# Three modulation tiles behind each projection in place of two, state-space steps to match, and constants loaded in two parts

## The chip, the cores and the metric

The kernel is one program on 1 core of a Trainium2 chip. The metric is the device time in microseconds (us) of one execution; lower is better. TensorE is called PE in the rows, VectorE DVE, ScalarE ACT, GpSimd POOL, and SyncE (which issues most of the transfers) SP. PEld is TensorE's loading of stationary operands.

## The reference: what is computed

Two transformer blocks run one after the other on 256 tokens of width 1024. The change touches only the start of the first block:

```
cs = silu(c)
mod = cs @ ada_w + ada_b              # ada_w: 1024 x 6144
sh1, sc1, g1, sh2, sc2, g2 = split(mod, 6)
h = rms_norm(x, norm1_g) * (1 + sc1) + sh1
u, q, k_cmp, v_cmp, k_slc, k_win, v_slc, v_win, gates, ... = h @ w_in
...                                    # state-space mixer on u: 32 groups, 64 states, a scan over 256 tokens
...                                    # compressed keys and values: gelu(blocks @ w1) @ w2
```

The second block has a modulation of the same shape, silu(c_2) and silu(c_ctx_2) times w_mod_2 (1024 x 6144). Its columns and the last four sixths of `mod` are needed only much later, so the kernel computes all of them here, as filler between the projections. After this stage come attention, the merging of the two branches, a mixture of experts (32 experts), and the second block with a mixture of experts of its own, which takes the larger part of the time.

## The kernel before

Every engine has an instruction stream of its own, written out in Python. The streams are tied by semaphores: `mark` counts an event up and `nth` gives the count that a waiting engine needs. The order on each engine is the order of the code, and nothing on an engine passes an instruction that waits.

**Weights.** All weights come through a ring of 12 slots of 1 MB (`RING`). The list `chunks` gives the order; `load` on SyncE waits until chunk i minus 11 has been counted as freed, and issues chunk i. First come eight chunks of modulation group 0. Then, for the 12 projections of the list `IN1` (u 0, u 1, q 0 to 3, kcmp, vcmp, kslc, kwin, vslc, vwin; below they are iterations i = 0 to 11), one chunk of `w_in` each, and behind each from i = 1 on two modulation chunks. Then a small chunk `ng`, two modulation chunks, four chunks `cw1` of the compression, and the last 16 modulation chunks. There are 40 modulation chunks in this filler, number f being k = f % 8 of group g = 1 + f // 8.

**Modulation on TensorE.** `modulation(g, k)` adds chunk k into bank 3 with four matmuls of 32 columns by 512. The sum over k = 0 to 7 is one group; ScalarE copies it out of bank 3 in `mod_rows(g)`, and TensorE turns it later in `turn_modulation(g)`. There is one bank for it, so the first matmul of the next group waits for that copy:

```
if k == 0 and g >= 1:
    pe.wait_ge(emptied, nth(emptied, ("mod rows", g - 1)))
```

**State-space steps.** The mixer has 16 steps j. `ssm_step()` on TensorE issues the input half `ssm_in(j)` of the next step and the output half `ssm_out(j)` of an earlier one, which runs two steps behind. Between them VectorE does the products and the scan of step j (L1923 to L1936), for which ScalarE makes sines (`sines()`, L1499 to L1502). ScalarE runs two calls of `sines()` ahead of TensorE's steps, and for want of buffers its call number j waits for VectorE's result of step j - 2:

```
act_.wait_ge(madeV, nth(madeV, ("fr", j)))
if j >= 2:
    act_.wait_ge(madeV, nth(madeV, ("s", j - 2)))
```

Before the change, TensorE does in each iteration from i = 2 on: the projection (L464, 128x128 by 128x256), two modulation chunks, one step, and at i = 3, 6 and 9 a second step right behind the first. ScalarE does in the same iteration: the copy of the projection out of its bank (`take`), its share of the two modulation chunks (`mod_rows` after k = 7, `mod_columns` at k = 2), and one or two calls of `sines()`.

**After the projections.** TensorE does `ng`, two modulation chunks and a step; the compression matmuls (hidR); four chunks and a step; hidT; four chunks and a step; kc; the last eight chunks; the turning of group 5; and what is left of the steps. Then VectorE adds the skip term (yD, L1939), and attention begins with two `scores` and the `router_constant`.

**Constants.** `K` is one tile of 1876 columns, loaded by one transfer at the start (938 KB); the three packs of parameters, which TensorE turns first, stand behind the constants in it. VectorE makes 16-bit copies of the identity and of two masks as its first work.

Of the kernel before, what the change touches and what calls it, by code (L numbers as in the profile page):

```python
# [19 lines left out]
P = 128  # L20
# [62 lines left out]
CONST_ARRAY = constants()  # L83
NCONST = CONST_ARRAY.shape[1]
# [22 lines left out]
def packed(I):  # L107

    packs = np.zeros((P, 3, P), np.float32)

    def rows(pk, at, name):
        a = I[name].reshape(-1, P)
        packs[at:at + len(a), pk, :] = a

    for at, name in ((0, "ada_b"), (48, "norm1_g"), (56, "norm2_g"), (64, "final_g"), (72, "nsa_cmp_pos"), (104, "c"),
                     (112, "c_2"), (120, "c_ctx_2")):
        rows(0, at, name)
    for at, name in ((0, "b_mod_2"), (48, "g_pre_mix_2"), (56, "g_post_mix_2"), (64, "g_pre_ffn_2"), (72, "g_post_ffn_2")):
        rows(1, at, name)
    for at, name in ((0, "ssm_lam_re"), (16, "ssm_lam_im"), (48, "ssm_d")):  # L120
        rows(2, at, name)
    packs[32:48, 2, :] = np.repeat(I["ssm_log_dt"].reshape(16, 2), 64, axis=1)

    ssm = np.zeros((P, 1536), np.float32)
    for n, name in enumerate(("ssm_c_re", "ssm_c_im")):
        c = I[name].reshape(4, P, 64).transpose(1, 0, 2)
        ssm[:, 512 * n:512 * n + 512] = np.concatenate([c, c], 2).reshape(P, 512)
    for n, name in enumerate(("ssm_b_re", "ssm_b_im")):
        ssm[:, 1024 + 256 * n:1280 + 256 * n] = I[name].reshape(16, P, 16).transpose(1, 0, 2).reshape(P, 256)

    by_rows = lambda a: a.reshape(-1, P, a.shape[-1]).transpose(1, 0, 2)
    tab = np.zeros((P, NTABLES), np.float32)
    tab[:, 0:288] = np.concatenate([by_rows(I["moe_w_group"]), by_rows(I["moe_w_expert"])], 2).reshape(P, 288)
    tab[:, 288:544] = by_rows(I["w_router_2"]).reshape(P, 256)
    tab[:, 544:800] = by_rows(I["nsa_cmp_w2"].reshape(512, HD)).reshape(P, 256)
    tab[:, 800:864], tab[:, 864:928] = I["g_qnorm_2"], I["g_knorm_2"]
    tab[0, 928:996] = np.concatenate([I["moe_b_group"], I["moe_b_expert"], I["b_router_2"]])
    return np.concatenate([CONST_ARRAY, packs.reshape(P, 3 * P)], 1), ssm, tab


class Counts:
# [18 lines left out]
def program(nc, A, const, ssm, tables, out, known):  # L160
# [3 lines left out]
    with ExitStack() as ctx:  # L164
# [3 lines left out]
        def sem(name):  # L168
            return ctx.enter_context(nc.semaphore(name))
# [7 lines left out]
        K = sb("consts", [P, NCONST + 3 * P])  # L177

        def cst(name, a=None, b=None):
            at, n = CONST[name]  # L180
            return K[:, at + (a or 0):at + (n if b is None else b)]

        packs = K[:, NCONST:NCONST + 3 * P].rearrange("p (a b) -> p a b", b=P)
        ring = sb("ring", [P, RING, SLOT])
        xT = sb("xT", [P, KD, T])
        hT = sb("hT", [P, KD, 2 * T])
# [9 lines left out]
        tab = sb("tables", [P, NTABLES])  # L196
# [155 lines left out]
        def mod_chunks(f, n):  # L352

            for i in range(f, min(f + n, 40)):
                mod_chunk(1 + i // 8, i % 8)
# [6 lines left out]
        for i, (n, c, at) in enumerate(IN1):  # L362
            chunk((n, c), wcols("w_in", at, at + 256), KD, 256)
            if i >= 1:
                mod_chunks(2 * i - 2, 2)
        chunk(("ng", 0), A["w_in"][:, 2560:2608].rearrange("(k p) c -> p k c", p=P), KD, 48)
        mod_chunks(22, 2)
        for kv in range(2):
            w = A["nsa_cmp_w1"][kv].rearrange("(c p) h -> p c h", p=P)
            for c in range(2):  # L370
                chunk(("cw1", kv, c), w[:, 8 * c:8 * c + 8, :], 8, 256)
        mod_chunks(24, 16)
        for c in range(4):
            chunk(("mga", c), wcols("w_in", 3120 + c * 256, 3376 + c * 256), KD, 256)
            chunk(("mgs", c), wcols("w_in", 4144 + c * 256, 4400 + c * 256), KD, 256)
# [46 lines left out]


        const_in = sem("constants_in")
        tables_in = sem("tables_in")
        ssm_loaded = sem("ssm_loaded")
        ctx_in = sem("ctx_in")
# [43 lines left out]

        @block.sync
        def _(sp):
            sp.dma_start(K[:, :], const[:, :]).then_inc(const_in, 16)

            for i in range(n1):
                key, src, shape = chunks[i]
                load(sp, key, i, src, shape)
                if key == ("u", 0):
                    sp.dma_start(arena[:, 1024:2560], ssm).then_inc(ssm_loaded, 16)  # L480
                if i == RING - 1:
                    sp.dma_start(tab[:, :], tables).then_inc(tables_in, 16)
# [101 lines left out]
        def _(pe):  # L584
# [149 lines left out]
            for i, (n, c, _) in enumerate(IN1):  # L734
                if n in ("u", "q"):
                    projT(n, c)
                elif n in ("kcmp", "vcmp", "kslc", "kwin"):
                    projT(n, 0)
                else:
                    projN(n, 256)  # L740
                freeing()
                if i == 1:
                    ssm_matrices()
                if i >= 1:
                    modulations(2)
                if n != "u":
                    ssm_step()
                    if i % 3 == 0:
                        ssm_step()
            projN("ng", 48)  # L750
            freeing()
            modulations(2)
            ssm_step()

            pe.wait_ge(emptied, nth(emptied, ("p1", turn[0] - 1)))
# [5 lines left out]
                              start=c == 0, stop=c == 15)  # L761
            last.then_inc(filled, mark(filled, "hidR"))
            freeing(4)
            modulations(4)
            ssm_step()
            pe.wait_ge(madeA, nth(madeA, "hidR"))
            for m in range(2):
                last = transpose(ps[:, 1, m * P:(m + 1) * P], hidR[:, m * P:(m + 1) * P])
            last.then_inc(filled, mark(filled, "hidT"))
            modulations(4)  # L770
            ssm_step()
            pe.wait_ge(madeA, nth(madeA, "hid"))
            pe.wait_ge(tables_in, 16)
# [5 lines left out]
                    last = mm(ps[0:NCMP, 1, g * HD:(g + 1) * HD], hid[:, m, 64 + g * NCMP:64 + (g + 1) * NCMP], w2c[:, 1, m, :],  # L779
                              start=m == 0, stop=m == 1)  # L780
            last.then_inc(filled, mark(filled, "kc"))
            modulations(8)
            turn_modulation(5)
            while done_j[1] < 16:
                ssm_step()
# [612 lines left out]
        def _(act_):  # L1398
# [107 lines left out]
            for i, (n, c, _) in enumerate(IN1):  # L1506
# [24 lines left out]
                    take(lambda b: copy((vslc if n == "vslc" else vwin)[:, :, :], two(b)))  # L1531
                if i == 1:
                    ssm_matrices()
                if i >= 1:
                    modulations(2)
                sines()
                if n != "u" and i % 3 == 0:
                    sines()
            take(lambda b: a(gates[:, :, :], b[:, 0:96].rearrange("p (a b) -> p a b", a=2), ACT.Sigmoid))
            modulations(2)  # L1540
            sines()

            act_.wait_ge(filled, nth(filled, "hidR"))
            a(hidR, ps[:, 0, 0:256], ACT.Gelu_apprx_tanh).then_inc(madeA, mark(madeA, "hidR"))
            modulations(4)
            sines()
            act_.wait_ge(filled, nth(filled, "hidT"))
            copy(hid.rearrange("p a b -> p (a b)"), ps[:, 1, 0:256]).then_inc(madeA, mark(madeA, "hid"))
            modulations(4)
            sines()  # L1550
            act_.wait_ge(filled, nth(filled, "kc"))
            copy(kcT, ps[:, 0, 0:60])
            copy(vcN[0:NCMP, :, :].rearrange("p a b -> p (a b)"), ps[0:NCMP, 1, 0:256]).then_inc(madeA, mark(madeA, "kc"))
            modulations(8)
            mod_columns(5)
            while nsin[0] < 16:
                sines()
# [244 lines left out]
        def _(v):  # L1802
# [28 lines left out]
            V.memset(cpad, 0.0)  # L1831
            v.wait_ge(const_in, 16)
            V.tensor_copy(ident16, cst("ident"))
            V.tensor_copy(causal16, cst("causal"))
            V.tensor_copy(cmpmask16, cst("cmpmask"))

            v.wait_ge(madeA, nth(madeA, "cols"))
            tt_(csil[:, :], csil[:, :], cols[:, 0, 104:128], ALU.mult)
# [44 lines left out]
            tt_(sm(12), sm(12), sm(10), ALU.mult)  # L1883
            step(tt_(sm(13), sm(14), sm(10), ALU.mult))
            b3 = lambda x: x.rearrange("p (j h) -> p j h", h=16)
            v.wait_ge(ssm_loaded, 16)
            cr_, ci_ = B(sm(12), 16), B(sm(13), 16)
            tmp = b3(sa[:, 0, :])
# [506 lines left out]
```

## Time and profile before

| | |
|---|---|
| median of 3 runs | 2052.98 us (2050.46 to 2053.23) |
| the profiled execution's own time | 2053.45 us |
| its span, first to last instruction | 2051.7 us |
| mean granted TensorE clock | 0.959 of full |
| TensorE busy | 1832.5 us (89%) |
| bytes moved | 626.77 MB, mean 305 GB/s |
| first projection begins | 33.30 us |
| attention of the first block begins | 214.72 us |

The stage that the change touches is the first tenth of the span. What lies behind attention's start does not depend on it except through the moment at which it begins. A time in the rows is microseconds from the start of the span.

### The profile page before, as it was taken

The numbers are of one execution on the slowest core, as the hardware profiler recorded it, in microseconds if no ns is written. First come the engines' busy times: TensorE is split into PE (matmuls) and PEld (weight loads), VectorE is DVE, ScalarE is ACT, GpSimd is POOL, SyncE is SP. The second block draws the span as 40 slices with busy tenths as digits, with TensorE's granted clock in tenths as the row PEclk, the third lists the DMA queues.
The fourth block names the chain that finished last, engine by engine and source line by source line (L and its number), as shares of the span: only waits on it lengthen the run. The fifth ranks groups of instructions, "written<-read, shape, count | busy, mean of one in ns | idle before, by whom it ended". The sixth has DMA issues, their size and how long they took to land.

```text
span 2051.7 us, 27907 instructions
## 1 busy us (share of the span) xinstructions
PE 1832.5 (89%) x10699; PEld 1006.3 (49%) x10700; DVE 527.4 (26%) x1211; ACT 390.7 (19%) x905; POOL 50.2 (2%) x109
## 2 busy tenths in 40 slices
PE   6999899978667889999978999889988999989887
PEld 4665677855344566777844333333333333323332
DVE  3676332131111133232431111111111111111112
ACT  3132454021011130244020111111100111101111
POOL 0040000000000010010010000000000000000000
PEclk9999899998888999999989999999999999999999
DMA  9968622418999662232435999999999899999997
GB/s 399 403 230 346 271 82 84 162 63 334 394 411 409 267 215 87 65 100 98 152 149 208 416 417 417 417 417 418 416 416 419 323 418 417 416 417 417 416 416 297
DMA packets 108632, 626.77 MB, mean 305 GB/s; under 512 B 11200, under 2 KB 15296, under 8 KB 50080
## 3 DMA queue, kind: packets, MB, share of 16 engines
q1 hardware_dynamic: 106688, 620.10, 75.1%
q0 software_dynamic: 1584, 4.33, 1.3%
q8 instruction: 70, 1.15, 0.2%
q10 hardware_dynamic: 272, 1.05, 0.1%
q14 instruction: 18, 0.15, 0.0%
HBM read 624.39 MB, written 1.05 MB: 305 GB/s over the span
## 4 chain that ended last, share of the span: by engine, by line
PE 62%; DMA 20%; SPq 10%; issue 4%; DVE 2%; ACT 1%; DVEq 0%; ACTq 0%
PE ps L464 59%; DMA ring<-in_w_gu_dram 15%; SPq L517 5%; SPq L520 4%; PE ps L592 2%; DMA ring<-in_moe_w_gate_dram 1%; DMA ring<-in_w_dn_dram 1%; DMA ring<-in_ada_w_dram 1%; DMA ring<-in_w_mod_dram 1%; DMA ring<-in_moe_w_down_dram 1%; ACT arena L1403 1%; PE ps L839 0%; SPq L490 0%; SPq L421 0%; ACT hT L1730 0%
## 5 line engine op out<-in xcount | busy, mean ns | idle before, releaser
L464 PE MATMUL ps<-ring,arena 128*64 128x512 f32 (+2 forms) x5376 | 898.8, 558 | 123.7 <-issue 59.1
L464 PEld LDWEIGHTS ps<-ring,arena 128*64 128x64 f32 (+1 forms) x5376 | 291.7, 131 | 671.4 <-issue 482.2
L464 PE MATMUL ps<-arena 64*128 64x512 f32 (+11 forms) x1494 | 262.2, 417 | 36.7 <-ACT arena L1403 15.5
L464 PE MATMUL ps<-hT,ring 128*128 128x256 f32 (+1 forms) x960 | 237.2, 402 | 2.3 <-DVE hT L1864 2.3
L464 PEld LDWEIGHTS ps<-hT,ring 128*128 128x128 f32 x960 | 180.5, 192 | 58.8 <-issue 33.6
L464 PEld LDWEIGHTS ps<-arena 64*128 64x128 f32 (+7 forms) x1494 | 128.2, 159 | 154.5 <-issue 97.0
L2212 DVE TENSOR_SCALAR arena<-ps 128x512 f32<-128x512 f32 (+1 forms) x34 | 23.0, 676 | 535.3 <-PE ps L464 535.3
L1403 ACT ACTIVATE arena<-ps 128x256 f32<-128x256 f32 (+5 forms) x191 | 104.3, 570 | 267.7 <-PE ps L592 134.0
L1669 ACT ACTIVATE arena<-ps,mod,gain 128x128 f32<-128x128 f32 x176 | 66.1, 458 | 425.3 <-PE ps L464 425.3
L1681 ACT ACTIVATE arena<-arena 128x512 f32<-128x512 f32 (+1 forms) x44 | 25.3, 575 | 601.7 <-DVE arena L2212 400.7
L464 PEld LDWEIGHTS ps<-arena,hN 128*128 128x128 f32 x960 | 116.3, 200 | 42.2 <-issue 16.3
L464 PE MATMUL ps<-arena,hN 128*128 128x128 f32 (+1 forms) x960 | 124.8, 287 | 10.3 <-DVE arena L2159 5.7
L464 PE MATMUL ps<-ring,hT 128*128 128x256 f32 (+2 forms) x416 | 83.5, 380 | 5.8 <-ACT hT L1743 5.8
L592 PE MATMUL ps<-consts,arena 128*128 128x128 f32 x522 | 73.7, 278 | 9.2 <-DVE arena L2218 6.2
L464 PEld LDWEIGHTS ps<-ring,hT 128*128 128x128 f32 (+1 forms) x416 | 70.6, 187 | 19.3 <-issue 8.3
L2199 DVE COPY arena<-ps 128x512 f32<-128x512 f32 x34 | 23.5, 692 | 214.1 <-PE ps L464 214.1
L464 PE MATMUL ps<-arena,ring 128*128 128x256 f32 x352 | 76.5, 380 | 0.7 <-ACT arena L1403 0.7
L592 PEld LDWEIGHTS ps<-consts,arena 128*128 128x128 f32 x522 | 60.1, 142 | 31.9 <-issue 15.0
L464 PEld LDWEIGHTS ps<-arena,ring 128*128 128x128 f32 x352 | 66.7, 190 | 10.3 <-ACT arena L1403 0.9
L1576 ACT ACTIVATE arena<-ps,stat 128x15 f32<-128x15 f32 (+3 forms) x128 | 56.0, 447 | 79.3 <-DVE stat L1960 79.3
L1960 DVE TENSOR_REDUCE stat<-ps 128x2 f32<-128x1024 f32 (+3 forms) x40 | 36.7, 917 | 129.4 <-PE ps L464 129.4
L464 PE MATMUL ps<-hN,ring 128*128 128x256 f32 x256 | 56.4, 380 | 0.0
(286 smaller groups left out, 876.1 us busy)
## 6 DMA issues: line engine op xcount, KB each, us to landing
ring<-in_w_gu_dram SPq DMA_DIRECT2D x256, 1024.0 KB, 20.3
ring<-in_w_dn_dram SPq DMA_DIRECT2D x128, 1024.0 KB, 23.1
ring<-dense_dram SPq DMA_DIRECT2D x56, 1024.0 KB, 12.2
ring<-in_moe_w_gate_dram SPq DMA_DIRECT2D x32, 1024.0 KB, 8.2
ring<-in_moe_w_up_dram SPq DMA_DIRECT2D x32, 1024.0 KB, 16.0
ring<-in_moe_w_down_dram SPq DMA_DIRECT2D x32, 1024.0 KB, 14.6
ring<-in_ada_w_dram SPq DMA_DIRECT2D x24, 1024.0 KB, 18.5
ring<-in_w_mod_dram SPq DMA_DIRECT2D x24, 1024.0 KB, 8.5
```

Of the source, the lines that this page charges most:

```text
L464: ins = nc.tensor.matmul(*a, start=start, stop=stop, **k)
L517: sp.dma_start(ring[:, i % RING, :], src).then_inc(full[i % RING], 16)
L520: sp.dma_start(slot_ap(i, (2, D)), src).then_inc(full[i % RING], 16)
L592: return nc.tensor.transpose(dst, src, ident[0:src.shape[0], 0:src.shape[0]])
L1403: return a(dst, src, ACT.Copy, scale=scale)
L1576: last = a(e_[:, s * nk:s * nk + m], ps[:, bank, at:at + m], ACT.Exp, bias=stat[:, i % 2, s:s + 1], accum_out=stat[:, i % 2, 4 + s:5 + s])
L1669: last = a(dst[:, d, :], ps[:, bank, k * P:(k + 1) * P], ACT.Identity, scale=gs[:, d:d + 1], bias=sh[:, d:d + 1])
L1681: a(sg[:, 0:w], glu[:, 0:w], ACT.Sigmoid, scale=1.702 if n == 2 else 1.0).then_inc(s["sig"], 1)
L1960: V.tensor_reduce(dst, sc[:, :, :, 0:m], AX.X, ALU.max, negate=True).then_inc(madeV, mark(madeV, ("mx", n, i)))
L2199: V.tensor_copy(dst, ps[:, 3, :]).then_inc(s["ys"], 1)
L2212: ts(glu[:, 0:w], ps[:, 1, 0:w], 7.0, None, ALU.min).then_inc(s["glu"], 1)
```

## The change

Three modulation chunks follow each projection (33 in all) and three follow `ng`; two each follow hidR and hidT, and the eight behind kc are gone. In the odd iterations i = 3, 5, 7, 9 and 11 there is a second state-space step, ahead of the modulation chunks; the second steps behind the first at i = 3, 6 and 9 are gone. TensorE, ScalarE and the list of chunks follow the same order. The packs are moved to the front of `K`; a first transfer takes columns 0 to 639 (packs, identity, ones), and a second, behind the first projection's chunk, the other 1236. VectorE makes the two masks' copies later and waits for the second transfer there.

```diff
-    return np.concatenate([CONST_ARRAY, packs.reshape(P, 3 * P)], 1), ssm, tab
+    return np.concatenate([packs.reshape(P, 3 * P), CONST_ARRAY], 1), ssm, tab
...
-                mod_chunks(2 * i - 2, 2)
+                mod_chunks(3 * i - 3, 3)
         chunk(("ng", 0), A["w_in"][:, 2560:2608].rearrange("(k p) c -> p k c", p=P), KD, 48)
-        mod_chunks(22, 2)
+        mod_chunks(33, 3)
...
-        mod_chunks(24, 16)
+        mod_chunks(36, 4)
...
-            sp.dma_start(K[:, :], const[:, :]).then_inc(const_in, 16)
+            early = 5 * P
+            sp.dma_start(K[:, 0:early], const[:, 0:early]).then_inc(const_in, 16)
...
                 if key == ("u", 0):
+                    sp.dma_start(K[:, early:], const[:, early:]).then_inc(masks_in, 16)
                     sp.dma_start(arena[:, 1024:2560], ssm).then_inc(ssm_loaded, 16)
...
@@ TensorE
                 if i == 1:
                     ssm_matrices()
+                if n != "u" and i % 2 == 1:
+                    ssm_step()
                 if i >= 1:
-                    modulations(2)
+                    modulations(3)
                 if n != "u":
                     ssm_step()
-                    if i % 3 == 0:
-                        ssm_step()
             projN("ng", 48)
             freeing()
-            modulations(2)
+            modulations(3)
...
-            modulations(4)      # behind hidR, and again behind hidT
+            modulations(2)
...
-            modulations(8)      # behind kc
             turn_modulation(5)
...
@@ ScalarE
                 if i == 1:
                     ssm_matrices()
+                if n != "u" and i % 2 == 1:
+                    sines()
                 if i >= 1:
-                    modulations(2)
+                    modulations(3)
                 sines()
-                if n != "u" and i % 3 == 0:
-                    sines()
...
@@ VectorE
             V.tensor_copy(ident16, cst("ident"))
-            V.tensor_copy(causal16, cst("causal"))
-            V.tensor_copy(cmpmask16, cst("cmpmask"))
...
+            v.wait_ge(masks_in, 16)
+            V.tensor_copy(causal16, cst("causal"))
+            V.tensor_copy(cmpmask16, cst("cmpmask"))
             v.wait_ge(ssm_loaded, 16)
```

## Rows read from the trace of the kernel before

**Rows 1.** The page: busy time, share of the span and instructions by engine

```profile
PE 1832.5 (89%) x10699; PEld 1006.3 (49%) x10700; DVE 527.4 (26%) x1211; ACT 390.7 (19%) x905; POOL 50.2 (2%) x109
```

**Rows 2.** The chain that ended last, 0 to 400 us: start, us, what

```profile
5.12 22.97 DMA ring<-in_ada_w_dram
...
187.46 19.86 DMA ring<-in_w_mod_dram
```

**Rows 3.** TensorE in order of time: start, us, what, [idle before <-releaser]

```profile
33.30 15.82 PE L464 MATMUL ps<-hT,ring 128*128 128x256 f32 x64 [2.33 <-DVE hT L1864]
...
61.61 1.13 PE L464 MATMUL ps<-arena 32*128 32x256 f32 x4
...
71.62 2.12 PE L464 MATMUL ps<-arena 32*128 32x256 f32 x12
73.67 7.17 PE L464 MATMUL ps<-hT,ring 128*128 128x256 f32 x32
80.78 1.92 PE L464 MATMUL ps<-ring,arena 128*32 128x512 f32 x16
82.63 2.11 PE L464 MATMUL ps<-arena 32*128 32x256 f32 x8
84.67 7.17 PE L464 MATMUL ps<-hT,ring 128*128 128x256 f32 x32
...
202.38 1.06 PE L464 MATMUL ps<-ring,arena 128*32 128x512 f32 x8 [0.75 <-DMA ring<-in_w_mod_dram]
204.87 1.06 PE L464 MATMUL ps<-ring,arena 128*32 128x512 f32 x8 [1.43 <-DMA ring<-in_w_mod_dram]
207.36 1.84 PE L464 MATMUL ps<-ring,arena 128*32 128x512 f32 x8 [1.43 <-DMA ring<-in_w_mod_dram]
209.90 1.12 PE L592 MATMUL ps<-consts,arena 128*128 128x128 f32 x4 [0.70 <-ACT arena L1403]
210.95 1.93 PE L464 MATMUL ps<-arena 128*32 128x256 f32 x8
214.72 2.88 PE L464 MATMUL ps<-arena 128*128 128x30 bf16 x20 [1.84 <-issue]
```

**Rows 4.** TensorE in the first units of attention, in order of time

```profile
217.53 3.63 PE L464 MATMUL ps<-tables,mod 128*128 128x36 f32 x16
...
222.94 1.03 PE L839 MATMUL ps<-consts,arena 128*15 128x128 f32 x4 [1.21 <-DVE arena L1977]
...
238.24 0.60 PE L839 MATMUL ps<-consts,arena 128*15 128x128 f32 x4
...
253.15 0.60 PE L839 MATMUL ps<-consts,arena 128*15 128x128 f32 x4
...
267.19 0.60 PE L839 MATMUL ps<-consts,arena 128*15 128x128 f32 x4
```

**Rows 5.** VectorE in order of time: the first operation of steps 0, 2 and 3

```profile
62.77 0.69 DVE L1923 TENSOR_TENSOR arena<-ps,arena 128x512 f32<-128x512 f32 x1 [15.72 <-PE ps L464]
...
79.96 0.68 DVE L1923 TENSOR_TENSOR arena<-ps,arena 128x512 f32<-128x512 f32 x1
...
87.13 0.68 DVE L1923 TENSOR_TENSOR arena<-ps,arena 128x512 f32<-128x512 f32 x1
```

**Rows 6.** ScalarE in order of time: a sine, and three kinds of copy

```profile
68.56 0.42 ACT L1499 ACTIVATE arena<-arena 128x256 f32<-128x256 f32 x1 [8.11 <-DVE arena L1936]
...
69.87 0.60 ACT L1403 ACTIVATE arena<-ps 128x512 f32<-128x512 f32 x1
...
102.87 2.40 ACT L1403 ACTIVATE hN<-ps 64x512 f32<-64x512 f32 x4 [1.09 <-PE ps L464]
...
209.25 0.60 ACT L1403 ACTIVATE arena<-ps 128x512 f32<-128x512 f32 x1 [10.03 <-PE ps L464]
```

**Rows 7.** Windows: engines' busy us (instructions), granted TensorE clock, DMA share, GB/s

```profile
30.00:36.50 6.50, 4.17 (x12) 3.11 (x13) 4.78 (x27) 1.58 (x3) 0.00 (x0) 0.50 1.02 419
...
207.70:228.00 20.30, 16.55 (x78) 11.14 (x71) 5.56 (x19) 7.92 (x30) 0.00 (x0) 0.50 1.01 420
```

More of the change, by code:

```diff
@@ L180, in cst @@
             at, n = CONST[name]
+            at += 3 * P
             return K[:, at + (a or 0):at + (n if b is None else b)]
-        packs = K[:, NCONST:NCONST + 3 * P].rearrange("p (a b) -> p a b", b=P)
+        packs = K[:, 0:3 * P].rearrange("p (a b) -> p a b", b=P)
         ring = sb("ring", [P, RING, SLOT])
@@ L424, in program @@
         const_in = sem("constants_in")
+        masks_in = sem("masks_in")
         tables_in = sem("tables_in")
@@ L769, in _ @@
             last.then_inc(filled, mark(filled, "hidT"))
-            modulations(4)
+            modulations(2)
             ssm_step()
@@ L1533, in _ @@
                     ssm_matrices()
+                if n != "u" and i % 2 == 1:
+                    sines()
                 if i >= 1:
-                    modulations(2)
+                    modulations(3)
                 sines()
-                if n != "u" and i % 3 == 0:
-                    sines()
             take(lambda b: a(gates[:, :, :], b[:, 0:96].rearrange("p (a b) -> p a b", a=2), ACT.Sigmoid))
-            modulations(2)
+            modulations(3)
             sines()
@@ L1544, in _ @@
             a(hidR, ps[:, 0, 0:256], ACT.Gelu_apprx_tanh).then_inc(madeA, mark(madeA, "hidR"))
-            modulations(4)
+            modulations(2)
             sines()
@@ L1548, in _ @@
             copy(hid.rearrange("p a b -> p (a b)"), ps[:, 1, 0:256]).then_inc(madeA, mark(madeA, "hid"))
-            modulations(4)
+            modulations(2)
             sines()
@@ L1553, in _ @@
             copy(vcN[0:NCMP, :, :].rearrange("p a b -> p (a b)"), ps[0:NCMP, 1, 0:256]).then_inc(madeA, mark(madeA, "kc"))
-            modulations(8)
             mod_columns(5)
```

## The prediction

> **What bounds the kernel now.** I read the page's engine table first: TensorE is busy 89% of the span [rows 1], so what TensorE waits for, and how long its own work takes, is what the time is made of. The share is an average over stages, so next I read the chain of work that ended last through the first 400 us. In the stage of the change two of its links are transfers [rows 2]: the eight chunks of group 0 until 28.1 us, and the last modulation chunks from 187.5 to 207.3 us. Between these the chain is TensorE alone. TensorE in order of time [rows 3] then shows where it stands still: not at all between 33.3 and about 201 us, then 0.75, 1.43 and 1.43 us for the last three chunks, 0.70 us for ScalarE's copy of bank 3, and 1.84 us before attention, where the profile names no engine; in the code it is the skip term yD, which waits for the last two state-space outputs (the row at 210.95, [rows 3]). The windows [rows 7] add that from 207.7 to 228 us TensorE had half of its clock (0.50, the 1.2 GHz level), after the three waits with little work between them. Last I read ScalarE and VectorE [rows 5, 6], which are busy 19% and 26%. They have room on average, but ScalarE spent 8.11 us of one iteration waiting for VectorE's step 0 before it could make a sine. Everything behind attention's start moves with it, one for one, so I add up how attention's start moves and then its first units.
>
> **Constants in two parts.** The first projection (33.30) hangs on the eighth chunk, and the transfers before it run without a break at 419 GB/s [rows 2, 7]. 1236 columns x 4 B x 128 partitions are 0.633 MB that no longer stand ahead of it: 0.633 MB / 419 GB/s = 1.5 us earlier. Below nothing it cannot go; above 1.5 us neither, as the whole queue's order is otherwise the same. The other work ahead of the first projection (x turned, squares, the norm) ended before that chunk. The second transfer stands ahead of the second projection's chunk, which then lands when it did before, and it is needed 7.1 us after the first starts, on a matmul stream that starts 1.5 us earlier: still there in time. The two mask copies on VectorE, two or three tenths, now lie ahead of the state-space matrices; VectorE had nothing to do from 47 to 62.77 us [rows 5], so they cost nothing; without that cover they would cost some 0.4 us. Taken: **-1.5 us**.
>
> **The tail that goes.** With three chunks per projection, an iteration brings four chunks, 4 x 2.49 us (204.87 to 207.36, [rows 3]) = 10.0 us of transfer. TensorE needs 7.11 (73.67 to 80.78) + 3 x 0.93 (half of 80.78 to 82.63) + 2.04 (82.63 to 84.67) = 11.9 us in an even iteration and one step more, 13.9, in an odd one. So the transfers stay ahead and the ring stays full. The slots for the four compression chunks and the last four modulation chunks come free in iterations 10 and 11, some 30 us ahead of their use (the second half of i = 10, 13.9 + 5 for i = 11, then ng, three chunks and a step); at 2.49 us, or even half as much again, eight chunks are in by then. The three waits for transfers go: -(0.75 + 1.43 + 1.43) = **-3.6 us**. The wait for the copy (0.70) and that for yD (1.84) go too, since the last output half is now issued ahead of kc; in their place TensorE will wait about 0.5 us for ScalarE's copies of kc and of the last columns: **-2.0 us**. The half clock on the last chunk (1.84 against 1.06) and on its four transposes (1.12 against 0.60, [rows 3, 4]) goes: **-1.3 us**. The two output halves at 210.95 ran side by side at half clock in 1.93 us; apart and at full clock they take 2 x 0.98: nothing.
>
> **Steps apart.** At i = 3 the two steps stood side by side: two input halves and one output half in 2.05 us (71.62 to 73.67), where one input half alone takes 1.05 (61.61 to 62.66, the start of what follows) and a whole step 2.04. Apart they take 3.1: **+1.0 us**. No other pair gains or loses, as there an output half lay between.
>
> **The wait that is new.** A group of modulation ends with f = 7, 15, 23, 31. Two chunks per iteration put a whole projection between it and the next group's first chunk. Three put f = 7 and 8 in the same iteration (i = 3), f = 15 and 16 in i = 6, and f = 31 and 32 in i = 11; only 23 and 24 are still parted. There the next chunk stands behind ScalarE's copy of bank 3, and everything TensorE has left stands behind that chunk. ScalarE comes late to it. In i = 3 and i = 11 the new call of `sines()` stands ahead of the copy, and it waits for VectorE's result of the very step that TensorE issued just before. The rows of step 0 time this: the input half ends at 62.66, VectorE starts at 62.77, the sine at 68.56, the next ScalarE instruction at 69.87, and a copy of bank 3 takes 0.60 [rows 5, 6]; TensorE goes on 0.05 us later (209.85 to 209.90). So the bank is free 69.87 - 62.66 + 0.60 + 0.05 = 7.9 us after the input half's end. TensorE reaches its wait after two chunks (1.85) at i = 3, where there is no output half yet, and after 0.98 + 1.85 at i = 11: waits of **6.0** and **5.0 us**. At i = 6 no call stands ahead, but ScalarE is still in the second call of i = 5. Counting from the start of i = 5: the first input half ends at 7.11 + 1.05 = 8.2; VectorE begins at 8.3 and, its steps being 7.17 apart when it has no pause (79.96 to 87.13), begins the next at 15.4; the sine starts 5.8 later (62.77 to 68.56) at 21.2 and ends at 22.5; the four copies of kcmp take 2.40, the bank's copy 0.60: 25.6. TensorE is there after 13.9 + 7.11 + 0.93 = 22.0: **3.6 us**. Together **+14.6 us**. From below: nothing, if ScalarE were never late; but even with ScalarE free each boundary costs 0.7 us (the 0.70 of 209.90), so 2.1. From above: 3 x 7.9.
>
> To attention's start this makes -1.5 - 3.6 - 2.0 - 1.3 + 1.0 + 14.6 = +7.2 us.
>
> **The clock behind the new waits.** Before the first projection TensorE did 1.06 us of work between waits of 0.72 and 2.33 us, had half its clock from 30.0 to 36.5 us, and 64 matmuls took 15.82 us where 64 x 0.222 (7.11 / 32) = 14.2 would do [rows 3, 7]: 1.6 us lost. Each new wait can bring that. The bounds are nothing and half of 6.5 us = 3.25 each. I take 1.6 for two of the three, the longer ones: **+3.2 us** (0 to 9.8). The Trainium skill ("TensorE: Matmul & The Clock Gate", "Why this matters for your kernels") says that idle gaps between bursts of matmuls bring the lower clock back. By that page all three waits would, and the sum would be 1.6 us more. Rows 7 agree as to the last modulation waits, after which the clock fell.
>
> **Attention's first units.** From 214.72 to the first transposes at 222.94 was 8.2 us at half clock, with the router constants (16 matmuls, 3.63) ahead of them. At full clock scores and constants take about half, 4.1 us; ScalarE, which must still do the gelu and make the exponentials, needs 4 to 5 us: about 4.6, so -3.6. From 222.94 to 238.24 three units took 15.30 us, and the same three of the next head at full clock 14.04 (253.15 to 267.19, [rows 4]): -1.3 more if the clock is full. These pieces have few columns, and the clock may fall in them, so I take **-4.0 us** (-5.1 to -2.5).
>
> **Sum.** +7.2 + 3.2 - 4.0 = +6.4 us. Made against the profiled execution's own 2053.45 us (span 2051.7 and 1.75 around it) it gives 2059.85; that execution lay 0.47 above the median shown, so I say 2059.4 us.
>
> **Rivals.** *The new waits cost TensorE time but no clock, and attention starts at full clock*: +7.2 + 0 - 5.1 = +2.1, 2055.1 us. For it: the mean clock is 0.959, and waits are short; against it: 30 to 36.5 us. Chance 0.2. *ScalarE is not late* (this ends on the other side): the place is bank 3 at f = 8, 16 and 32. If the copy came at once, only 3 x 0.7 would be left: -7.4 + 2.1 - 4.0 = -9.3, 2043.7 us. The new waits and their clock decide together: under 11.4 us the change gains, over it loses. For it speaks that ScalarE is busy 19%; against it that it had been waiting 8.11 us for just this VectorE result. Chance 0.1. *Every new wait brings a long stretch of half clock, and attention too starts low*: +7.2 + 9.8 - 2.5 = +14.5, 2067.5 us. Chance 0.1. The forecast's own case has 0.6 and a range of its own of 2056 to 2064 us.
>
> **How the numbers follow.** A measurement of this kernel can tell about 0.2%, 4.1 us, from no change. Slower by more than that (over 2057.1) are nearly all of the forecast's case, 0.58, and the last rival, 0.1; within 0.2% are the first rival and the rest of the forecast's, 0.22; faster is the rival with ScalarE on time, 0.1. The range for 8 in 10 leaves out that one and a part of the last: 2053.5 to 2067 us.
>
> **What the profile after would show.** First projection at 31.8 us, not 33.3. TensorE idle before a modulation matmul, released by ScalarE's copy, near 73 us (6.0), 117 (3.6) and 188 (5.0), with a granted clock of 0.50 behind at least two; no wait for the modulation transfers near 200; attention at about 225 us instead of 214.7, its first transposes some 4.6 us later. The prediction is wrong if VectorE's result does not hold ScalarE in i = 3, 5 and 11, if the transfers do not keep ahead, or if the stretches behind attention's start do not simply move.

## The result and the profile after

The changed kernel took 2068.74 us (median of 4 runs, 2067.13 to 2070.72) against 2051.85 us of the kernel before in the same comparison (4 runs): ratio 1.0086, 95% interval 1.0073 to 1.0099, so 16.9 us slower. The forecast was slower, at 2059.4 us, with a range up to 2067.0: the sign is right, the size is off by 9.3 us, and the range ends 1.7 us too low. The profiled execution took 2069.31 us, with a span of 2067.5 us against 2051.7.

TensorE in order of time in the changed kernel, the rows that answer to [rows 3, 4]:

```profile
26.60 1.06 PE L466 MATMUL ps<-ring,arena 128*32 128x512 f32 x8 [1.42 <-DMA ring<-in_ada_w_dram]
...
31.50 16.08 PE L466 MATMUL ps<-hT,ring 128*128 128x256 f32 x64 [2.33 <-DVE hT L1864]
...
78.73 1.93 PE L466 MATMUL ps<-ring,arena 128*32 128x512 f32 x8 [5.80 <-ACT arena L1406]
80.60 3.92 PE L466 MATMUL ps<-arena 32*128 32x256 f32 x8
84.44 8.32 PE L466 MATMUL ps<-hT,ring 128*128 128x256 f32 x32
92.69 1.06 PE L466 MATMUL ps<-ring,arena 128*32 128x512 f32 x8
...
124.01 3.37 PE L466 MATMUL ps<-ring,arena 128*32 128x512 f32 x16 [3.92 <-ACT arena L1406]
127.31 2.31 PE L466 MATMUL ps<-arena 32*128 32x256 f32 x8
129.55 7.17 PE L466 MATMUL ps<-hT,ring 128*128 128x256 f32 x32
...
198.09 1.93 PE L466 MATMUL ps<-ring,arena 128*32 128x512 f32 x8 [4.96 <-ACT arena L1406]
199.96 3.92 PE L466 MATMUL ps<-arena 32*128 32x256 f32 x8
203.80 7.06 PE L466 MATMUL ps<-ring,hT 128*128 128x48 f32 x32
...
216.92 2.11 PE L466 MATMUL ps<-arena 32*128 32x256 f32 x8
...
234.29 1.72 PE L466 MATMUL ps<-arena 128*128 128x30 bf16 x20 [0.44 <-ACT mod L1406]
...
240.44 1.03 PE L842 MATMUL ps<-consts,arena 128*15 128x128 f32 x4 [1.21 <-DVE arena L1980]
...
254.90 0.60 PE L842 MATMUL ps<-consts,arena 128*15 128x128 f32 x4
```

Three idle times released by ScalarE's copy stand in it, 5.80, 3.92 and 4.96 us, where the prediction had 6.0, 3.6 and 5.0. No transfer is waited for behind the first projection. Attention begins at 234.29, not 214.72: 19.6 us later, where 10.4 was forecast. What the prediction missed is visible in the rows behind each wait: the step at 80.60 takes 3.84 us to the next row, and so does the one at 199.96, where [rows 3] has 2.04.

ScalarE in order of time, iteration 3 of the changed kernel, answers to [rows 6]:

```profile
70.06 0.60 ACT L1406 ACTIVATE arena<-ps 128x512 f32<-128x512 f32 x1
76.90 0.42 ACT L1502 ACTIVATE arena<-arena 128x256 f32<-128x256 f32 x1 [6.24 <-DVE arena L1939]
77.22 0.40 ACT L1503 ACTIVATE arena<-arena 128x256 f32<-128x256 f32 x1
77.69 0.42 ACT L1505 ACTIVATE arena<-arena 128x256 f32<-128x256 f32 x1
78.01 0.58 ACT L1406 ACTIVATE arena<-ps 128x512 f32<-128x512 f32 x1
```

The projection is copied at 70.06; then ScalarE stands 6.24 us for VectorE's result, makes the sine, and only then comes the copy of bank 3 (78.01) for which TensorE is waiting. That copy's input had been ready since about 73 us.

Windows over the three stretches that follow the waits, in the changed kernel (busy us of each engine, granted clock, DMA share, GB/s), answer to [rows 7]:

```profile
76.70:87.30 10.60, 8.57 (x24) 4.29 (x25) 5.80 (x13) 1.62 (x4) 0.00 (x0) 0.52 1.01 418
124.50:127.90 3.40, 3.40 (x18) 1.10 (x11) 0.00 (x0) 0.00 (x0) 3.40 (x15) 0.52 0.28 92
196.00:214.60 18.60, 16.51 (x68) 9.99 (x72) 5.94 (x13) 3.93 (x9) 0.00 (x0) 0.50 0.44 163
```

The clock is at its half level (1.2 GHz) through nearly all of each: 10.6, 3.4 and 18.6 us. The last one covers the whole of `ng` (203.80 to 210.79).

### The profile page after: what moved, and what is told of

Same layout as the page of the kernel before. It is cut to its first block, busy times and chain, and to the rows that moved or that the text cites. A ratio compares the mean times of both kernels' runs of the same rounds, so it can differ in the third digit from the quotient of the medians.

```text
span 2067.5 us, 27905 instructions
## 1 busy us (share of the span) xinstructions
PE 1839.8 (89%) x10697; PEld 1011.3 (49%) x10700; DVE 527.2 (26%) x1211; ACT 389.7 (19%) x904; POOL 50.5 (2%) x109
## 4 chain that ended last, share of the span: by engine, by line
PE 62%; DMA 17%; SPq 11%; issue 4%; DVE 2%; ACT 2%; DVEq 1%; ACTq 0%
PE ps L466 60%; DMA ring<-in_w_gu_dram 13%; SPq L521 7%; SPq L524 4%; PE ps L596 2%; DMA ring<-in_w_dn_dram 1%; DMA ring<-in_ada_w_dram 1%; ACT arena L1406 1%; DMA ring<-in_moe_w_down_dram 1%; DMA ring<-in_moe_w_gate_dram 1%; DVEq L1847 0%; PE ps L842 0%; ACT hT L1732 0%; SPq L422 0%; DVE arena L1932 0%
## 5 line engine op out<-in xcount | busy, mean ns | idle before, releaser
L1406 ACT ACTIVATE arena<-ps 128x512 f32<-128x512 f32 (+5 forms) x191 | 104.5, 570 | 258.7 <-PE ps L596 131.7
## 6 DMA issues: line engine op xcount, KB each, us to landing
ring<-in_ada_w_dram SPq DMA_DIRECT2D x24, 1024.0 KB, 21.4
```

Source lines behind the costliest of these rows:

```text
L1406: return a(dst, src, ACT.Copy, scale=scale)
```

## The experiments

Each is compared with runs of the kernel before on the same chip; that kernel's median there was 2049.86 us beside the first four kernels, 2050.13 beside the next four and 2050.75 beside the last four. A difference between two kernels of different groups is one between chips; where it matters, the ratios are given too. A profile is of one execution.

| kernel | median us | ratio to before (95%) |
|---|---|---|
| e1 constants split alone | 2049.98 | 0.9998 (0.9987 to 1.0008) |
| e2 copy before the sines | 2050.41 | 1.0002 (0.9990 to 1.0014) |
| e3 groups whole | 2041.67 | 0.9963 (0.9949 to 0.9976) |
| e5 three chunks, old steps | 2053.78 | 1.0024 (1.0012 to 1.0035) |
| e6 changed kernel again | 2069.16 | 1.0089 (1.0062 to 1.0116) |
| e7 copy first at i = 11 alone | 2056.11 | 1.0029 (1.0015 to 1.0043) |
| e8 copy first at i = 3 alone | 2062.91 | 1.0061 (1.0037 to 1.0085) |
| e9 ng behind its chunks | 2067.12 | 1.0079 (1.0055 to 1.0103) |
| e10 groups whole, old steps | 2044.47 | 0.9969 (0.9960 to 0.9979) |
| e11 before, new steps | 2051.57 | 1.0009 (0.9999 to 1.0019) |
| e12 copy before kcmp at i = 6 | 2065.94 | 1.0078 (1.0063 to 1.0092) |
| e13 groups whole, not split | 2041.60 | 0.9954 (0.9941 to 0.9966) |

My theory was that the loss sits wholly in the three waits for ScalarE and the half clock behind them. The rivals were that the three chunks or the moved steps are dear in themselves, and that narrow work, not the waits, brings the half clock.

### e2: ScalarE's copy ahead of the sines

```diff
-                if n != "u" and i % 2 == 1:
-                    sines()
                 if i >= 1:
                     modulations(3)
                 sines()
+                if n != "u" and i % 2 == 1:
+                    sines()
```

> The changed kernel, but in the odd iterations ScalarE's first sines stand behind its copy of the modulation rows, not ahead of it; TensorE's order is untouched. Theory (the new waits of 5.80 and 4.96 us are ScalarE held by VectorE's result, and the half clock behind them is their consequence): the waits at i = 3 and i = 11 shrink to about 0.7 us each, the one at i = 6 (3.92) stays, the 3.9 and 7.2 us lost to half clock behind the two go: 2069.3 - 5.1 - 4.3 - 3.9 - 7.2 = about 2049 us. Rival 1 (the boundary itself costs, whoever makes the copy, since there is one bank): 2069 us. Rival 2 (the half clock comes from the narrow state-space matmuls that now stand apart, not from the waits): only 9.4 us go, about 2060 us.

Measured: 2050.41 us, 18.7 us under the changed kernel's 2069.16 (e6; the kernel before beside the two had 2049.86 and 2050.13), from an exchange of two calls on an engine that is busy 19% of the time. By the two ratios (1.0089 and 1.0002) it is 17.8 us. TensorE's waits in order of time:

```profile
73.55 1.06 PE L466 MATMUL ps<-ring,arena 128*32 128x512 f32 x8 [0.81 <-ACT arena L1406]
...
115.00 3.64 PE L466 MATMUL ps<-ring,arena 128*32 128x512 f32 x16 [3.92 <-ACT arena L1406]
...
187.38 1.06 PE L466 MATMUL ps<-ring,arena 128*32 128x512 f32 x8 [0.78 <-ACT arena L1406]
```

Two of the waits shrink to 0.8 us, which one bank and a copy cost whoever makes it, and the one at i = 6, where the edit moves nothing, stays at 3.92. The chunks behind the short waits take 1.06 us, full clock. So the half clock is the waits' doing at these two places, and the rival that had only 9.4 us go is out. The Trainium skill ("TensorE: Matmul & The Clock Gate", "Architectural detail: the array is 16× 32×32, not 1× 128×128") calls ScalarE's queue strictly first in, first out. The trace agrees: the copy stood 5 us with its input ready behind a sine that waited.

### e7 and e8: the same at one place each

The diff is that of e2 with `i != 11` (e7) or `i != 3` (e8) added to the first condition, and the later call made for that i alone.

> The changed kernel with ScalarE's copy ahead of the sines in iteration 11 alone. What is to be told apart is the price of the third wait. Theory (half clock begun by that wait cannot end in the narrow matmuls of ng and costs 7.2 us more than before): 4.3 + 7.2 = 11.5 us under the changed kernel, and the clock full again before or soon behind ng. Rival (a wait costs itself and the 1.6 us of the prediction): 5.9 us under it.

> The changed kernel with ScalarE's copy ahead of the sines in iteration 3 alone. Theory (behind the first wait stand one step and a projection, and the clock is full again within the projection): 5.1 + 3.9 = 9.0 us under the changed kernel. Rival (as the prediction sized it): 6.7 us under it.

> The changed kernel once more, as the base of the three kernels beside it on the same chip, and to see whether the stretches of half clock repeat. Expected: 17 us (14 to 19) over the kernel before; the waits at i = 3, 6 and 11 at 5.8, 3.9 and 5.0 us; behind the third, half clock through the whole of ng.

The changed kernel again: 2069.16 us, 19.0 us over the kernel before, waits of 5.80, 3.91 and 4.96 us, and `ng` again at half clock throughout (7.06 us for its 32 matmuls). e7 is 13.0 us under it, near the 11.5 of the theory and far from the 5.9 that the prediction's sizing gives: the third wait is the dear one. In its profile the third place alone gives back 4.2 us of wait and 8.7 of clock, a longer stretch behind the second wait takes 3.3 again (below), and attention begins at 224.57 us, 9.7 earlier. e8 is 6.3 us under it by medians, nearer the rival's 6.7 than the theory's 9.0, but the intervals of the two ratios (1.0037 to 1.0085 and 1.0062 to 1.0116) can't tell these apart. Its profile speaks for the theory: attention begins at 226.15 us, with the first projection at 32.52. That is 193.6 us of stage against 202.8 in the changed kernel, 9.2 less, and the two profiled executions differ by 8.6 us (2060.72 and 2069.31). The one of e8 was the fastest of its four (2060.72 to 2063.83; e6 has 2066.32 to 2072.14).

In e7 the granted clock from 196.0 to 214.6 us is whole. Windows of e7:

```profile
124.50:134.50 10.00, 10.00 (x29) 5.09 (x22) 5.26 (x9) 0.00 (x0) 7.14 (x27) 0.50 0.83 333
196.00:214.60 18.60, 17.82 (x135) 10.50 (x136) 14.29 (x28) 4.81 (x9) 0.00 (x0) 1.00 0.99 382
```

In the same 18.6 us TensorE ran 135 matmul records, and 68 in the changed kernel. The first row shows the other side: behind the wait of 3.91 us the clock stayed at half for 10.0 us here and 3.4 us in the changed kernel, with the same wait and the same work. e7 differs from the changed kernel only at i = 11, later than this, so the difference is one between executions and not between kernels. From the end of the wait to the end of the next projection the changed kernel, e6 and e9 took 12.6 us, e8 12.3, e7 15.9 (123.84 to 139.77) and e2 15.1. So the price of a wait in clock is not one number.

### e9: ng behind its three chunks

```diff
-            projN("ng", 48)
-            freeing()
             modulations(3)
+            projN("ng", 48)
+            freeing()
             ssm_step()
```

The list of chunks and ScalarE's order are changed to match.

> The changed kernel with the three modulation chunks that follow ng moved ahead of it, in the list of chunks and on both engines; the three waits stay as they are. Theory (ng's 48-column matmuls, standing right behind the third wait and a step, are what keeps the half clock on): the chunks bring the full clock back before ng, half clock behind the third wait costs about 4 to 5 us in place of 8.6, and the kernel is 3 to 4 us under the changed one. Rival (the half clock lasts its time whatever runs in it): within 1 us of the changed kernel.

Measured: 2067.12 us, 2.0 us under e6, less than its interval can tell. The profile tells more. TensorE in order of time in e9, and under it the windows:

```profile
198.04 1.94 PE L466 MATMUL ps<-ring,arena 128*32 128x512 f32 x8 [4.96 <-ACT arena L1406]
...
208.22 3.77 PE L466 MATMUL ps<-ring,hT 128*128 128x48 f32 x32
...
230.91 1.72 PE L466 MATMUL ps<-arena 128*128 128x30 bf16 x20 [0.44 <-ACT mod L1406]
```

```profile
196.00:206.00 10.00, 7.96 (x27) 2.85 (x28) 4.06 (x9) 1.62 (x4) 0.00 (x0) 0.50 0.70 265
206.00:213.00 7.00, 7.00 (x56) 4.92 (x54) 1.83 (x5) 2.50 (x5) 0.00 (x0) 0.99 0.94 342
213.00:217.00 4.00, 4.00 (x19) 1.86 (x20) 3.68 (x7) 0.58 (x1) 0.00 (x0) 0.58 0.98 369
```

The wait is the same 4.96 us. The clock rises during the chunks, `ng` runs in 3.77 us instead of 7.06, and then the clock falls once more behind it. Attention begins 3.4 us earlier than in the changed kernel. The time decides nothing (3 to 4 us were expected, the rival had less than 1), but the profiles speak for the theory: `ng` took 7.06 us in all four kernels that have it right behind the third wait and a step (the changed kernel, e6, e8, e12), and 3.77 us here. So what stands behind a wait has a part in how long the half clock lasts. Attention's first units gave back a part: they ran with the clock low for longer (233 to 244 us, in windows of 1 us, against 237 to 244).

The fall behind `ng` has no wait ahead of it. The kernel before has one too, which the prediction did not use:

```profile
169.90:173.80 3.90, 3.90 (x22) 1.16 (x20) 2.76 (x8) 2.22 (x4) 0.00 (x0) 0.56 0.98 357
```

TensorE was busy all of this stretch and had been since 33.3 us; the clock fell in the last of `ng` (166.58 to 170.52). The stretch is in e1 as well. In e2, e3, e5, e7, e10, e11 and e13 the clock stayed full behind the same 32 matmuls. So the rival of the narrow work is half right: `ng` without a wait can bring the half clock, for some 3.4 us (3.90 us of window at 0.56), and does not do so in every kernel.

### e12: the third place, i = 6

```diff
                 elif n in ("kcmp", "vcmp"):
+                    if i == 6:
+                        modulations(3)
```

ScalarE's later `modulations(3)` is left out for i = 6.

> The changed kernel with one change in iteration 6: ScalarE's copy of the modulation rows stands ahead of its four copies of kcmp. Theory (the 3.92 us there are the end of a call of the sines and these copies, 2.40 us): the wait at i = 6 is 1.5 us, the other two stay at 5.80 and 4.96, and the kernel is 2.4 us under the changed one, up to 4 with the half clock behind it. Rival (the sines alone hold the copy): wait and time unchanged.

Measured: 2065.94 us, a wait of 1.49 us at i = 6, the other two 5.80 and 4.96. TensorE in order of time in e12:

```profile
78.80 1.94 PE L466 MATMUL ps<-ring,arena 128*32 128x512 f32 x8 [5.80 <-ACT arena L1406]
...
121.69 1.92 PE L466 MATMUL ps<-ring,arena 128*32 128x512 f32 x16 [1.49 <-ACT arena L1406]
...
194.12 1.94 PE L466 MATMUL ps<-ring,arena 128*32 128x512 f32 x8 [4.96 <-ACT arena L1406]
```

The wait is the 1.5 us that were expected, and the chunks behind it run at full clock (1.92 for two, against 3.37). The rival is out: the four copies of kcmp were 2.4 us of that wait. The time is 3.2 us under e6 by medians and 2.3 by ratios; 2.4 to 4 were expected, but the intervals overlap, so the time alone decides nothing.

### e5 and e10: the steps where they were

```diff
                 if i >= 1:
                     modulations(3)
                 if n != "u":
                     ssm_step()
+                    if i % 3 == 0:
+                        ssm_step()
```

In both kernels the step ahead of the chunks is taken out, and ScalarE's sines follow. e10 has in addition the whole groups of e3.

> The changed kernel with the state-space steps (and ScalarE's sines) where they were before: a second step behind the first at i = 3, 6, 9, two left for the end. The groups still end inside i = 3, 6 and 11. Theory (a group end inside an iteration costs little unless a call of the sines stands ahead of the copy): waits of about 0.7 us at i = 3 and 11, and 2 us at i = 6, where the four copies of kcmp stand ahead; no half clock but that behind ng: 2045 us, 2043 to 2049. Rival (the three chunks alone make the waits, with or without the moved steps): 2065 us or more.

> Whole groups (3, 3 and 2 chunks), constants split, but the state-space steps and sines where they were before the change. Theory (the moved steps cost 1.0 us on TensorE and pay at the end, where with old steps the last output waited 3.57 us for VectorE and yD 1.80 more, at half clock): about 7 us slower than the same kernel with the moved steps, which was 8.2 us under the kernel before; so 1 us under the kernel before, 2049 us where that has 2050. Rival (the steps are worth nothing where no transfer is late): 2041 us.

e5 took 2053.78 us, not 2045, and far from the rival's 2065. TensorE's waits in it:

```profile
71.95 1.06 PE L466 MATMUL ps<-ring,arena 128*32 128x512 f32 x8 [0.81 <-ACT arena L1406]
...
109.81 1.92 PE L466 MATMUL ps<-ring,arena 128*32 128x512 f32 x16 [2.21 <-ACT arena L1406]
...
176.19 1.06 PE L466 MATMUL ps<-ring,arena 128*32 128x512 f32 x8 [0.81 <-ACT arena L1406]
...
210.19 1.05 PE L466 MATMUL ps<-arena 128*32 128x256 f32 x4 [3.57 <-DVE arena L1939]
213.03 2.88 PE L466 MATMUL ps<-arena 128*128 128x30 bf16 x20 [1.80 <-issue]
```

The first three are as expected (0.7, 2, 0.7). What I had left out is the end: with the last chunks gone from behind kc, two steps are left with nothing to stand beside, TensorE waits 3.57 us for VectorE's last scan and 1.80 for yD, and starts attention at half clock. So the moved steps pay at the end for what they cost in the iterations. In e10, where eight chunks again stand behind the compression, these waits are 1.85 and 1.80 us:

```profile
207.13 1.05 PE L467 MATMUL ps<-arena 128*32 128x256 f32 x4 [1.85 <-DVE arena L1940]
209.98 2.87 PE L467 MATMUL ps<-arena 128*128 128x30 bf16 x20 [1.80 <-issue]
```

The kernel takes 2044.47 us: 6.3 us under the kernel before, so better than my 2049, and by the two ratios 0.06% slower than e3, which the intervals can't tell apart. The better comparison is e13, which has the moved steps (and the constants whole) and ran beside e10 on the same chip: 2041.60 us, 2.9 less. In the profiles attention's first transposes come at 218.19 us in e10, 212.47 in e13 and 211.44 in e3. So the moved steps are worth some 3 us there by medians and up to 6 by profiles, under the 7 expected and not nothing.

### e11: the kernel before with the new steps

> The kernel before (two chunks, 16 at the end, constants whole) with only the state-space steps and sines moved as in the change. Theory (the last modulation transfers still set the end of the stage at 207 us, but the two output halves and the wait for yD behind them go): attention's start 3.3 us earlier, 2046.7 us where the kernel before has 2050. Rival (double steps with VectorE's result ahead of ScalarE's copies of the projections stall TensorE here too): 2053 us or more.

The diff is the step part of the change on both engines, with two chunks. Measured: 2051.57 us, ratio 1.0009, no gain. TensorE's last waits for transfers in it:

```profile
207.88 1.94 PE L464 MATMUL ps<-ring,arena 128*32 128x512 f32 x8 [1.56 <-DMA ring<-in_w_mod_dram]
210.24 1.94 PE L464 MATMUL ps<-ring,arena 128*32 128x512 f32 x8 [0.42 <-DMA ring<-in_w_mod_dram]
212.89 1.12 PE L592 MATMUL ps<-consts,arena 128*128 128x128 f32 x4 [0.72 <-ACT arena L1403]
214.45 2.88 PE L464 MATMUL ps<-arena 128*128 128x30 bf16 x20 [0.44 <-ACT mod L1403]
```

Neither theory nor rival holds. There is no stall in the iterations and the two output halves are gone from the end, but the last chunk comes at 210.24, not 207.36: the unbroken run of the last transfers starts at 190.28 us in e11 and at 187.46 in the kernel before, 2.8 us later, each time right behind TensorE's work that freed a slot:

```profile
190.28 19.92 DMA ring<-in_w_mod_dram
```

More steps ahead of the chunks free the ring's slots later, and the last transfers are later by nearly as much as was saved: attention begins at 214.45 us instead of 214.72.

### e1 and e13: the constants

e1 is the kernel before with the constants' part of the diff alone; e13 is e3 without it.

> The kernel before with the constants in two parts and nothing else. Theory (the split is worth the 0.633 MB that no longer stand ahead of the first projection's last chunk): first projection at 31.5 us, and the rest moves with it until the last modulation transfers. These are bound by the order of transfers alone, so a part of the 1.5 us may be lost there: 2050.3 to 2051.8 us. Rival (the second transfer or the later mask copies cost something in their new place): 2053 us or more.

> Whole groups and moved steps, with the constants in one transfer as before. Theory (with no late transfer behind it the split is worth its 1.5 us, which the kernel before could not show, as its stage ends with the transfers): 1.5 us slower than with the split, so 6.7 us under the kernel before, 2043.3 us where that has 2050. Rival (the clock's phase swallows it): no difference, 2041.8 us.

e1: 2049.98 against 2049.86 us. e13: 2041.60, and e3 2041.67 on another chip. Neither shows a gain, but with intervals of 2 us and more to either side neither can exclude one of 1.5 us. TensorE in order of time in e1:

```profile
27.26 1.93 PE L466 MATMUL ps<-ring,arena 128*32 128x512 f32 x8 [1.42 <-DMA ring<-in_ada_w_dram]
29.91 1.11 PE L596 MATMUL ps<-consts,arena 128*128 128x128 f32 x4 [0.72 <-ACT arena L1407]
33.36 15.73 PE L466 MATMUL ps<-hT,ring 128*128 128x256 f32 x64 [2.33 <-DVE hT L1866]
...
207.64 1.93 PE L466 MATMUL ps<-ring,arena 128*32 128x512 f32 x8 [1.43 <-DMA ring<-in_w_mod_dram]
```

The eighth chunk is 0.9 us earlier than in the kernel before, but it and the transposes run at half clock (1.93 for one chunk), so the first projection begins at 33.36, and the end of the stage hangs on the transfers, at 207.64, as before. The first projection began at 31.50 us in the changed kernel, and at 32.87 (e6, the same kernel), 31.75 (e2), 32.74 (e3), 31.40 (e5) and 33.36 (e1), all with the constants split. The eighth chunk began at 26.53 to 26.77 us in all of these but e1, so in them it is the clock that takes a part of the 1.5 us, another one each time. Over the eleven profiles with the split the mean start is 32.1 us, over the three without it (the kernel before, e11, e13) 33.2: it is worth about 1 us at this place.

### e3: groups whole

```diff
+        PER = [0, 3, 3, 2, 3, 3, 2, 3, 3, 2, 3, 3]
...
                 if i >= 1:
-                    modulations(3)
+                    modulations(PER[i])
...
             projN("ng", 48)
             freeing()
-            modulations(3)
+            modulations(2)
...
-            modulations(2)      # behind hidR and behind hidT
+            modulations(4)
```

> The changed kernel with 3, 3 and 2 modulation chunks behind three projections in turn (30 behind the projections, 2 behind ng, 4 behind hidR, 4 behind hidT), so that every group of eight ends with an iteration; all else as changed. Theory (everything the change lost it lost at group ends within an iteration): no wait for ScalarE's copy, no wait for the modulation transfers, attention's start near 205 us, 2041 us. Rival 1 (three chunks per projection or the steps apart are dear in themselves): 2050 us or more. Rival 2 (with eight chunks behind the compression the transfers are late again): waits of 2 to 5 us near 200 us, 2043 to 2046 us.

Measured: 2041.67 us, ratio 0.9963, 8.2 us under the kernel before, and faster than it and the changed kernel. One window of e3 over the stage, and the row at which attention starts (TensorE in order of time):

```profile
49.00:206.00 157.00, 156.82 (x926) 98.70 (x924) 106.55 (x218) 40.06 (x92) 22.62 (x64) 1.00 0.90 352
```

```profile
206.26 1.72 PE L467 MATMUL ps<-arena 128*128 128x30 bf16 x20 [0.44 <-ACT mod L1407]
```

TensorE works 156.82 of 157 us at full clock, waits for no transfer and for no copy, and attention begins at 206.26 us (205 expected). Both rivals are out: three chunks and steps apart cost nothing to speak of when no group ends inside an iteration, and eight chunks behind the compression arrive in time. Of the gain, 1.6 us are the half clock behind `ng` that the kernel before has and e3 has not; no edit aimed at it, so they are luck.

## Why the prediction was right in sign and wrong in size

**The new waits: right.** Forecast 6.0, 3.6 and 5.0 us, in all 14.6; measured 5.80, 3.92 and 4.96, in all 14.7. Cause and place are shown by e2, e7, e8 and e12.

**The tail: right.** The three waits for transfers (3.6 us), the copy's 0.70 and yD's 1.84 are gone, 0.44 is left of the 0.5 allowed.

**Constants: right at the chunk, not in the time.** The eighth chunk moved from 28.13 to 26.60, the forecast 1.5 us, and in the profile the first projection from 33.30 to 31.50. The next profile of the same kernel has 32.87, so the 1.8 us are in part luck. Alone the split gained nothing that the runs tell (e1, e13).

**The clock behind the new waits: the step that failed.** The prediction took 1.6 us for two of three waits, 3.2 us, with 9.8 as its upper bound. Measured against the same work at full clock: behind the first wait 78.73 to 92.69 is 13.96 us where 0.93 + 2.04 + 7.11 = 10.1 would do, 3.9 lost; behind the second 124.01 to 129.55 is 5.54 where 3.9 would do, 1.6 lost; behind the third 198.09 to 216.92 is 18.83 us, and e7 has the same work in 10.17 (197.03 to 207.20), 8.7 lost, of which the kernel before had lost some 1.6 in its own `ng`. Together 12.6 us, not 3.2, and above the bound. Two things were wrong in it. The price was taken from one place, the first projection, where dense wide matmuls follow and the clock came back 3.2 us after the restart. Here it came back after 8.6 us in the first case (a step stands between), and in the third only behind `ng`; e9, against the four profiles with `ng` right behind, speaks for the order of the work behind the wait as the reason. What in that work keeps the clock low stays open. And the bound of half of 6.5 us was the length of that one stretch, which bounds nothing elsewhere; 10.6 and 18.6 us were measured. The trace on which the prediction rests had, besides, a stretch at half clock with no wait at all (169.90 to 173.80), so gaps alone were not all that brings it.

**Attention's first units: mis-sized, small.** From attention's start to the first transposes 6.15 us instead of 8.22, so -2.1 where -3.6 was taken, and three units in 14.46 (240.44 to 254.90) instead of 15.30, -0.8. Together -2.9 for the forecast's -4.0. The clock fell once more in them, as the prediction had feared.

**The sum.** From the first projection to attention's start, 202.79 us against 181.42, so 21.4 more. The terms give 14.7 (waits) + 12.6 (clock) - 5.7 (old waits, less 0.44) - 1.3 (half clock at the old end) + 1.0 (steps apart, as forecast: at i = 3 they take 3.1 us in e3 and 2.05 in e10) + 0.3 (the first two projections, 16.08 for 15.82) = 21.6. Less 1.8 for the earlier start and 2.9 in attention this is 16.9; the two spans differ by 15.8. The last microsecond lies behind and is not explained; from attention's first transposes to the end the fourteen profiled executions took 1823.9 to 1830.8 us (1828.8 before, 1827.1 in the changed kernel), with the same code behind it, and executions of the kernel before alone beside the first four experiments range over 10 us (2045.83 to 2056.0).

The rival nearest to what happened was the last one, every new wait with a long half clock, 2067.5 us, to which I gave 0.1. It came near the sum with waits and clock of nearly the right total, but spread evenly over the three places, which they are not.

The Trainium skill ("TensorE: Matmul & The Clock Gate", "Why this matters for your kernels") holds that idle gaps between bursts bring the lower clock back. The runs agree for every wait of 3.9 us and more; behind single waits for ScalarE of 0.8, 1.49 and 2.21 us the clock stayed full. Gaps are not the only thing that brings it: it fell behind `ng` with no gap at all in the kernel before, e1 and e9.

## What to carry to other kernels

Where one accumulator serves several groups in turn, count at which place in the loop a group ends, and what stands ahead of the releasing copy on the engine that makes it: a wait hidden in a lightly used engine (busy 19% of the program, 43.5 of the stage's 202.8 us) cost some 18 us here, and an exchange of two calls gave it back. Place the group's end so that an independent piece of work follows it, as e3 does; then the change was worth 8.2 us. A stall on TensorE is to be priced with the work behind it: the wait of 5.0 us cost 4.2 us more than the 0.8 that one bank costs anyway, and 8.7 us of clock, when a step and the 48-column matmuls of `ng` followed.

## What the runs showed of the hardware that was not expected

The same wait of 3.9 us at i = 6 was followed by half clock for 3.4 us in the changed kernel and for 10.0 us in e7, with the same instructions behind it and no edit ahead of it. And the stretch of 18.6 us at half clock in the changed kernel was full of work: TensorE was busy 16.51 us of it. `ng` ran wholly at half clock again in e6, e8 and e12, and did not in e9, where three modulation chunks stood ahead of it. And the clock fell to half behind `ng` with TensorE busy without a gap, in the kernel before (3.9 us of window at 0.56), e1 and e9, but not in seven others with the same matmuls.
